# TensorE takes the stage steps of an even slot and of the next odd slot together, behind the odd slot's unit

## The reference

```python
def layer_ab(x, ...):        # gated linear attention (4 heads) and forgetting attention (8 heads)
    h = rms_norm(x, norm_g); g_q, g_k, ... = split(h @ w_in)
    return x + concatenate([o_gla, o_fox]) @ w_out
def layer_c(x, ...):         # S5: a diagonal complex state space, 128 groups of 16 channels
    u, gate = split(rms_norm(x, norm_g) @ w_in)
    z = gelu(s5_ssm(u, ...)); z = z * sigmoid(z @ glu_w + glu_b)
    return x + (z * silu(gate)) @ w_out
def second_block(x, ...):    # two layers: SSD (16 heads), a convolution branch, attention (4 heads)
    for l in range(2):
        proj = rmsnorm(x, norm_w[l]) @ w_in[l]
        x = x + concatenate([y_ssd, y_cfm, y_att]) @ w_out[l]
```

## Time and profile before

| | us |
|---|---|
| three runs | 3979.3, 3985.6, 3987.74 |
| median | 3985.6 |
| the profiled execution, its own time | 3974.32 |
| its span | 3972.5 |
| PE busy | 3635.0 |
| DVE busy | 2121.8 |
| ACT busy | 1301.9 |
| mean granted clock of PE | 0.96 |

### The profile page before, as it was taken

One profiled execution on the slowest core, in us unless ns is written; L12 is line 12 of the kernel. 1 busy time (PEld: TensorE's weight loads), 2 busy tenths in 40 slices (PEclk: granted clock), 3 DMA queues, 4 the chain that ended last, 5 costly groups with the idle time before them and its releaser, 6 DMA issues.

```text
span 3972.5 us, 44433 instructions
## 1 busy us (share of the span) xinstructions
PE 3635.0 (92%) x16658; PEld 2891.5 (73%) x16658; DVE 2121.8 (53%) x3119; ACT 1301.9 (33%) x2022; POOL 150.1 (4%) x100
## 2 busy tenths in 40 slices
PE   7899999878879999999998989998899999999799
PEld 6677777666668777778887877676677877677567
DVE  6745545555554433443424466566655466566654
ACT  4233324333333222332314223423433223432432
POOL 2000000000011000000005000000001000000000
PEclk9999999989999999999999999999999999999899
DMA  4333334355564444544543343334436343334345
GB/s 149 101 107 115 115 106 159 131 177 177 175 217 158 152 137 140 159 165 169 194 162 134 116 146 125 106 125 144 149 125 225 124 149 134 104 117 157 118 137 185
DMA packets 283061, 574.66 MB, mean 145 GB/s; under 512 B 43984, under 2 KB 100064, under 8 KB 282336
## 3 DMA queue, kind: packets, MB, share of 16 engines
q1 hardware_dynamic: 282848, 571.82, 43.2%
HBM read 440.65 MB, written 131.07 MB: 144 GB/s over the span
## 4 chain that ended last, share of the span: by engine, by line
PE 45%; issue 24%; DVE 15%; ACT 7%; DMA 6%; DVEq 2%; POOLq 1%; SPq 1%; ACTq 0%
PE bank L529 28%; PE bank L528 9%; DVE weights_low L463 3%; ACT weights_high L390 3%; DMA arena<-in_s_bc 2%; DVE arena L1948 1%; POOLq L449 1%; ACT arena L1890 1%; PE bank L2225 1%; DMA arena<-fm_b 1%; DVE arena L1812 1%; PE bank L1052 1%; DMA convert_in<-x 1%; PE bank L960 1%; DVE act_low L512 1%
## 5 line engine op out<-in xcount | busy, mean ns | idle before, releaser
L529 PE MATMUL bank<-act_high,weights_high 128*128 128x512 f32 x3328 | 1356.7, 408 | 43.9 <-DVE stream_out L501 24.1
L463 DVE TENSOR_TENSOR weights_low<-weights_raw,weights_high 128x1024 fp32r<-128x1024 f32 x528 | 657.3, 1245 | 1377.0 <-ACT weights_high L390 1374.5
L529 PE MATMUL bank<-act_low,weights_high 128*128 128x512 f32 x3328 | 1323.2, 398 | 0.0
L390 ACT ACTIVATE weights_high<-weights_raw 128x1024 fp32r<-128x1024 f32 x528 | 557.7, 1057 | 1653.2 <-PE bank L529 1239.7
L529 PE MATMUL bank<-act_high,weights_low 128*128 128x512 f32 x3328 | 897.9, 390 | 0.0
L529 PEld LDWEIGHTS bank<-act_high,weights_high 128*128 128x128 f32 x3328 | 645.1, 194 | 195.1 <-DVE act_low L512 34.8
L529 PEld LDWEIGHTS bank<-act_low,weights_high 128*128 128x128 f32 x3328 | 643.7, 193 | 132.3 <-issue 3.6
L529 PEld LDWEIGHTS bank<-act_high,weights_low 128*128 128x128 f32 x3328 | 626.5, 188 | 131.3
L528 PE MATMUL bank<-weights_high,act_high 128*128 128x512 f32 x896 | 363.8, 406 | 27.1 <-DVE stream_out L476 18.0
L528 PE MATMUL bank<-weights_high,act_low 128*128 128x512 f32 x896 | 356.6, 398 | 0.0
L528 PE MATMUL bank<-weights_low,act_high 128*128 128x512 f32 x896 | 237.6, 389 | 0.0
(11 more groups left out here) (319 smaller groups left out, 3252.2 us busy)
## 6 DMA issues: line engine op xcount, KB each, us to landing
weights_raw<-in_w_all SPq DMA_DIRECT2D x528, 512.0 KB, 3.3
convert_in<-mix SPq DMA_DIRECT2D x80, 256.0 KB, 3.9
fm_b<-stream_out SPq DMA_DIRECT2D x72, 256.0 KB, 2.4
mix<-arena SPq DMA_DIRECT2D x64, 256.0 KB, 4.2
x_part<-stream_out SPq DMA_DIRECT2D x48, 256.0 KB, 2.3
residual_in<-x_part SPq DMA_DIRECT2D x12, 1024.0 KB, 6.6
x<-stream_out SPq DMA_DIRECT2D x48, 256.0 KB, 2.5
convert_in<-x SPq DMA_DIRECT2D x48, 256.0 KB, 4.4
```

What stands on the lines that cost most here:

```text
L390: e.activation(WH[:, t % 3, :], RAW[:, t % 3, :], ACT.Copy).then_inc(wh_ready, 1)
L463: e.tensor_tensor(WL[:, t % 3, :], RAW[:, t % 3, :], WH[:, t % 3, :].bitcast(F32), ALU.subtract).then_inc(wl_ready, 1)
L529: return e.matmul(bank[s][:, :], a[:, s * P:(s + 1) * P], h, start=start, stop=stop)
```

## The change

PE's loop over the slots no longer calls `take(t)` behind every unit. Behind an even slot's unit it goes straight on to the next unit; behind an odd slot's unit it takes the pieces of the even slot before and then its own. Nothing is added and nothing left out, and the other engines' programs are the same.

```diff
@@ -2590,7 +2590,10 @@
                 if t == 2:
                     e.wait_ge(const_in, 80)
                 unit_pe(e, t)
-                take(t)
+
+                if t % 2:
+                    take(t - 1)
+                    take(t)
             finish()
```

## The result

The changed kernel takes 4160.6 us (median of 4 runs, 4156.2 to 4163.9), the kernel before 3983.8 on the same chips (3979.3 to 3987.7). The ratio is 1.0443, 95% interval 1.0425 to 1.0462: **177 us slower**. The forecast was 4064, slower by 79, and its range ended at 4135. The direction was right, the size less than half of what came, and the time lies outside the range.

A forecast was written before the change was run, and what follows sets the result against it. PE was taken as the bound, idle for only 337 us of 3972.5. Stage terms -14 + 7 + 16 + 12 + 22 + 46 - 10 = +79 gave 4053, and the runs' median 11 above that 4064 us, range 3975 to 4135.

The forecast's parts named there:

- SSD's second L1919 waits 2.0, the first pair 4: SSD heads: the second L1919 of a pair has 2.0 us exposed, a layer's first pair 4; stage total +22 us.
- which is 1.1 per pair of 19 us, and goes: SSD heads: today's idle time, 9.6 of 160 us, disappears, leaving net 0.9 to 1.1 per pair, +8 for 8 pairs.
- Attention: Attention stage, +46 us: +21 from L2219 behind the head before's sum, the rest from output, last transposes and smaller terms.
- GLA: Slots 17 to 72, +16 us: heads 0 and 2 +11, heads 1 and 3 -9, squares +4, ends of passes +10.
- s5w and fox, -14: Slots 75 to 136: L960's shorter waits and clock gains outweigh new waits at L966 and fox's short trips, -14 us.
- 3.3 exposed, in one pair less: +22: s5w: in seven pairs L966 directly follows L960 and waits for L908, 3.3 us exposed, one pair less, +22 us.
- I take 2 each back: -12: s5w and fox: six long waits gone give back 2 us of half clock each, -12 us.
- Half clock stays near today's amount: Whole kernel: time at half clock hardly changes; the forecast is wrong if granted clock, 0.96 today, falls below 0.93.
- Rival 2: Whole kernel: every new wait costs clock as well, about 60 times 1.7 us, 100 more, 4165 us; chance 0.12.
- Rival 1: Whole kernel: trips inside pairs are covered and even slots' waits shrink, -95 us, 3890 us; chance 0.11.
- Rival 3: Whole kernel: waits only move, each pair giving back what its even slot saves; within 8 us of 3985.6; chance 0.07.
- The ends of passes: Small terms per stage where a late step delays the next unit's evacuation, such as S5's 3 x 5.1 = +15 us.

The follow-up runs named there:

- lab_short_idle: Kernel before, plus PE waits in slots 219 to 254: 1.9 us behind every second unit, 1.9 behind every unit, 3.7 behind every second; granted clock 0.89 and 0.88 in the last two.
- lab_narrow_work: Kernel before, plus small matmuls in S5's form (partly 64-column weights) in slots 219 to 254: joined behind every second unit 155.6 us at 0.77, singly 129.2 at 0.97.
- lab_small_work: Kernel before, plus small full-weight matmuls in slots 219 to 254, no waits: 48 behind every unit, 96 or 48 behind every second; rows of 10.6 and 21.4 us kept 1.00.
- waits_inside_pairs: Kernel before, plus step pairs with a wait of about 1.9 us inside, slots 219 to 254: SSD's form granted 0.97, small full-width matmuls 0.76, 64-column weights 0.96.
- lab_idle: Kernel before, plus PE waits in slots 219 to 254: 5.0 us behind every second unit, 9.9 behind every second, 5.0 behind every; next unit took 7 to 8.3 us.

## Why the prediction was right in direction and wrong in size

- **The waits of even slots shrink by a unit: right.** L960 was to fall to about 55 and is 52.1; L1547's share in even slots went (33.2 to 12.9, and 6.7 at L1553 behind ACT's copies). S5's idle time came out as summed, +6.6 beside +7.
- **SSD's second L1919 waits 2.0, the first pair 4: right.** Its row now, in the pair of slots 322 and 323:

```profile
2551.48 1.16 PE L1919 MATMUL bank<-tri,arena 128*128 128x128 f32 x8
...
2552.57 2.37 PE L1928 MATMUL bank<-arena 128*64 128x512 f32 x8
...
2552.67 1.13 DVE L1943 TENSOR_SCALAR arena<-bank,arena 128x128 f32<-128x128 f32 x4 [4.81 <-PE bank L1919]
...
2556.15 0.65 ACT L1882 ACTIVATE arena<-arena 128x512 f32<-128x512 f32 x1
...
2556.85 1.16 PE L1919 MATMUL bank<-tri,arena 128*128 128x128 f32 x8 [1.92 <-ACT arena L1882]
```

  14 pairs of 1.92 and two of 4.22 make the 35.3 of the waits. Wrong was "which is 1.1 per pair of 19 us, and goes": 8.4 of 10.4 us at L1928 stayed. The first unit behind these slots waits 5.1 a layer, 1.2 before, where the forecast had a gain of 1. Idle time rose by 33, not 22; the upper bound of 40 had been this case.
- **Attention: right.** L2219 stands at 74.5, about 75 was given. The wait in heads 2 and 3 is 7.67, where 7.5 was worked out:

```profile
2990.43 1.02 PE L2263 MATMUL bank<-arena,ones 128*128 128x512 f32 x2
...
2999.56 1.11 PE L2219 MATMUL bank<-ident,arena 128*128 128x128 f32 x4 [7.67 <-DVE arena L2371]
```

- **GLA, +18.8 beside +16: near, and in part by luck.** The scores' waits in heads 0 and 2 grew by 8.5, where +11 was put; heads 1 and 3 gave back 3.3, where 7 of waiting was put. The two errors cancel. L1052 keeps 29.2 under two names, not 26.
- **s5w and fox, -14: wrong by 38.** "L966, which has none now" was misread, it had 3.6 in three waits; and the "3.3 exposed, in one pair less: +22" came out as 31.6 in eight waits, up to 4.3. L908 does not need the pair's first step, but its queue does. Slot 95 in the changed kernel:

```profile
779.79 0.69 DVE L1449 TENSOR_TENSOR arena<-bank,arena 128x512 f32<-128x512 f32 x1 [2.17 <-PE bank L1377]
...
780.57 1.36 DVE L905 TENSOR_TENSOR arena<-arena 128x1152 f32<-128x1152 f32 x1
...
784.78 3.57 PE L966 MATMUL bank<-arena 128*16 128x128 f32 x16 [4.21 <-DVE arena L908]
```

  DVE held L905 to L908 behind L1449, which waited 2.17 for PE's fox output of the same pair. Fox's own short trips came to 17 (L1347, L1341), not 8. And "I take 2 each back: -12" of half clock was +9.7. Of the nine waits of L960 in even slots three went and six only became shorter, while eight pairs with a wait at L966 inside came. How much of the 9.7 those cost isn't shown.
- **"Half clock stays near today's amount": the step that failed most.** It was +75.2 where the sum held about -8 (-12 in s5w, -2 in GLA, +6 in attention), 83 of the 111 us that the forecast missed; idle time was 119 against some 97, and the saving on changes between units and steps 4 against 10. The forecast read the clock only as something that waits cost, from the earlier trace rows, and gave the new waits inside pairs no price in clock but attention's. Both were wrong. In S5, whose idle time grew by 6.6 alone, the steps one after the other without a unit between lost 26.7, and 19.4 of it went with the same waits when the narrow products were widened. In the SSD heads idle time grew by 33 and the clock's cost by 17.5, where no term stood; without a wait, steps of that form kept 1.00.
- **Rival 2** gave 4165 us, nearly the time measured, with a chance of 0.12; that it came so near is in part luck. Its 100 us for waits stand against 75 in all, of which at least 19 of S5's 27 hang on its narrow products and not on waits, and its base, the forecast, had too little idle time; the granted clock was 0.938, above the 0.93 that was set as its mark. What the Trainium skill, "TensorE: Matmul & The Clock Gate", section "A second HAM failure mode: psum-queue depth-cycling", says of frequent short idle pieces that bring the low clock back is borne out by lab_short_idle (0.98 with 1.9 us behind every second unit, 0.89 behind every one). That rows without idle time in the profile do it too (0.77) is what the runs add.
- **Rival 1** (the trips are covered) fell at L966 (31.6), L1919 (35.3), L2219 (74.5) and the second scores of a head (L1052 behind L1182, 5.4). Only at L1948 did it hold: the second L1928 of a pair mostly waits for nothing, 8.4 us in four waits. **Rival 3** fell with the time.
- **The ends of passes.** Single ones were sized well (5.1, measured 5.37, 5.30 and 5.05), but the forecast went stage by stage and had them as small terms, some 40 together. The waits for an evacuation grew by 55. Taken away, the pairs at the ends are worth 77, the clock behind them included.

Not settled: how the clock's cost in the convolution (15) and s5w (10) divides between waits and thin rows, and what makes the 7 us of S5's that widening left. For SSD's form the wait is shown to be needed, though the imitation kept 0.97 where the changed kernel's heads had 0.95; for the others nothing was tried.

## What to carry to other kernels

A dense stream between two small steps is worth two things: it hides the trip to the other engines and back, and for steps like S5's it keeps the matrix engine's clock up (0.97 singly, 0.77 joined). So price a reordering by distances, each step to the next one that needs it and each row of thin steps to the next dense work, and look at the ends of passes first, where a late step stands ahead of the evacuation in its queue. To hide waits, move every step later by the same part of a unit instead of joining them: half a unit was worth 2.3% here, while joining cost 4.4%. More is not always better: five sixths of a unit was worth 1.7%.

## What the runs showed of the hardware

- The granted clock falls without idle time that the profile shows. S5's mix of full and 64-column weights with 64 moving columns was granted 0.77 in rows of 12.0 to 13.8 us behind every second unit, and 0.97 in rows of 4.9 behind every one (lab_narrow_work).
- 96 small matmuls with full weights in a row, 21.4 us, kept 1.00 (lab_small_work); 60 of them with one wait of 1.9 us in the middle, 19.6 to 21.5 us with the wait, were granted 0.76 together with the units between (waits_inside_pairs).
- A wait of 5.0 and one of 9.9 us behind every second unit cost nearly the same clock, 2.3 and 2.4 us of the next unit (lab_idle). Waits of 1.9 us behind every unit or 3.7 behind every second, the same idle time, were granted 0.89 and 0.88 (lab_short_idle).
